# FFN down projection: 2x2 blocks as seven block products of sums in place of eight, four quads in each pair of column chunks

## The chip, the cores and the metric

One Trainium2 chip, one core. The time is the device time of one execution in microseconds (us). Before the change three executions took 1940.80, 1941.48 and 1941.52 us, median 1941.48.

## The reference, cut to what matters

A block of a language model on x [1, 256, 2048] in float32: an FFN, a mixer (sparse attention beside a gated delta rule), a second FFN, each followed by a layer norm over a residual.

```python
def swiglu(x, w_gate, w_up, w_down):            # w_gate, w_up [2048, 5632], w_down [5632, 2048]
    return (jax.nn.silu(x @ w_gate) * (x @ w_up)) @ w_down

h = layer_norm(DEEPNORM_ALPHA * h + 0.5 * swiglu(h, ffn1_w_gate, ffn1_w_up, ffn1_w_down), ln1_g, ln1_b)
mix = hybrid_mixer(h, w_in, ...)
h = layer_norm(DEEPNORM_ALPHA * h + mix, ln2_g, ln2_b)
h = layer_norm(DEEPNORM_ALPHA * h + 0.5 * swiglu(h, ffn2_w_gate, ffn2_w_up, ffn2_w_down), ln3_g, ln3_b)
```

The change touches the two products with w_down: [256, 5632] x [5632, 2048] each.

## The kernel before, in words

All weights stream through the core once, as units: two K tiles (256 rows of the weight) by 512 columns, 512 KB. SyncE loads a unit into one of eight slots of `raw` (`load_unit`, L316), waiting until the unit that held the slot has been split. ScalarE (ACT) copies it, rounded, to `whi` (`split_hi`, L351); VectorE (DVE) subtracts that from `raw` into `wlo` (`split_lo`, L358); both have three slots. TensorE (PE) multiplies the unit: for each half of the 256 tokens and each K tile three matmuls, activation high by weight high (L370), high by low (L371), low by high (L372), with the activations as stationary operand and 512 weight columns moving. That is 12 matmuls a unit. Each engine walks through the stream in one order written out by hand; semaphores count (`hi_done`, `lo_done`, `unit_used`), and `Stream` works out which count each wait needs. `ring_place` gives the slot of a unit: u % 8 for `raw`; for the three split slots u % 3, but behind the middle of a phase with a remainder the ring turns, so that the next phase can begin in slot 0. There some slots are used again after two units and not three.

In a phase "ffn down" the activations lie in `hT` (44 K tiles, high and low parts, features on the partitions). For each of four chunks of 512 columns 22 units accumulate into `acc0` (two PSUM banks, one for each token half), and DVE adds the banks to `resid` (L843) and takes statistics for the layer norm (L854) between the low parts of the next chunk. The first chunk begins while the last 512 columns of hT are still made: gated by up (L759), transposes on PE behind unit 3 (L740), copy and subtraction to hT (L746, L750). In the last chunk the last six units are split into `edge` slots of their own, and PE takes them first for token half 0 and then for half 1 (`exit_units`), so that the norm of the first tile (`exit_tiles`: resid, statistics, norm_columns L622 and L626, transpose L461, xT L474) runs beside half 1. The `edge` slots lie over parts of hT that are used up by then. Before `exit_tiles` DVE splits three units of the next phase. GpSimd loads the norm's gains over the first part of hT and computes the inverse root.

Of the kernel before, what the change touches and what calls it, by code (L numbers as in the profile page):

```python
# [19 lines left out]
P = 128  # L20
# [6 lines left out]
LEAD = 2  # L27
# [9 lines left out]
class Phase:  # L37


    def __init__(self, name, iters, units, width):  # L40
        self.name, self.iters, self.units, self.width = name, iters, units, width

# [13 lines left out]
class Stream:  # L56
# [14 lines left out]
    @staticmethod  # L71
    def uses(ph, s):
        return sum(ring_place(u, ph.units, RAW_SLOTS) == s for u in range(ph.units))
# [5 lines left out]
    def loaded(self, p, it, u):  # L79

        n = self.phases[p].units
        if u >= n:
            it, u = it + 1, u - n
        s = ring_place(u, n, RAW_SLOTS)
        earlier = sum(ring_place(v, n, RAW_SLOTS) == s for v in range(u))
        return it * (16 * self.uses(self.phases[p], s)) + 16 * (self.loads[p][s] + earlier + 1)

    def freed(self, p, it, u, slots):

        n = self.phases[p].units  # L90
# [7 lines left out]
        else:  # L98
            prev = [v for v in range(n) if ring_place(v, n, slots) == s]
            c = prev[-1] - n + 1 if prev else -n  # L100
            if not over:
                if p > 0:
                    m = self.phases[p - 1].units
# [8 lines left out]
def hybrid_block(nc, x, x_t, ffn1_w_gate, ffn1_w_up, ffn1_w_down, ln1_g, ln1_b, w_in, q_norm_g, kv_norm_g,  # L112
# [29 lines left out]
    DOWN_U = FT // UNIT_KT  # L142
    A_ITERS, C_ITERS = 2, 3
    A_W, C_W = A_COLS // A_ITERS, Z_COLS // (C_ITERS + 1)
    B_ITERS = 3 * BW // BANK
    F1GU, F1D, WA, WZ, WB, WC, WQI, WUQ, WO, F2GU, F2D = range(11)
# [3 lines left out]
        Phase("ffn1 down", OUT_CHUNKS, DOWN_U, BANK),  # L150
# [8 lines left out]
        Phase("ffn2 down", OUT_CHUNKS, DOWN_U, BANK),  # L159
    ])  # L160

    n0 = {F1GU: 0, F1D: 11, WA: 15, WZ: 16, WB: 17, WC: 23, WQI: 26, WUQ: 30, WO: 32, F2GU: 36, F2D: 47}
    n1 = {F1GU: 0, WA: 11, F2GU: 12}

    with ExitStack() as ctx:
# [20 lines left out]
        gated = mz("gated", 88, [P, T, BANK])  # L186
        ln_g = mz("ln_g", 0, [P, D])
# [135 lines left out]
        def split_place(p, it, u):  # L323

            n = st.phases[p].units
            if p in EXITS and isinstance(it, int) and it == st.phases[p].iters - 1:
# [16 lines left out]

        def split_hi(act, p, it, u):
            n, w = st.phases[p].units, cut_width(p, it, u)
            hi, _, s, free = split_place(p, it, u)
            r = ring_place(u % n, n, RAW_SLOTS)
            act.wait_ge(raw_loaded[r], st.loaded(p, it, u))
# [4 lines left out]
        def split_lo(dve, p, it, u):  # L353
            n, w = st.phases[p].units, cut_width(p, it, u)
            hi, lo, s, _ = split_place(p, it, u)
            r = ring_place(u % n, n, RAW_SLOTS)
# [60 lines left out]

        def halves(bank):
            return bank.rearrange("p (k s) -> p k s", k=2)
# [9 lines left out]
        def first_units_pe(pe):  # L429

            for v, (c, k) in enumerate(FIRST):
                if v == 0:
                    pe.wait_ge(sem("xT_lo_first"), 1)
# [137 lines left out]
        def to_xT_act(act, q):  # L571
            if q == 0:
                first_hi(act, slice(0, UNIT_KT), sem("x_first"), sem("xT_hi_first"))
# [18 lines left out]
        def to_xT_dve(dve, q):  # L592
            if q == 0:
                first_lo(dve, slice(0, UNIT_KT), sem("xT_hi_first"), 1, sem("xT_lo_first"))
# [44 lines left out]
        def exit_tiles(dve, e, p, scale):  # L639

            c, units = OUT_CHUNKS - 1, KU if p == WO else DOWN_U
            resid_tile(dve, p, c, scale, units, 0)
# [9 lines left out]
            resid_tile(dve, p, c, scale, units, 1)  # L652
# [3 lines left out]
            else:  # L656
                last_pieces(dve, 1)

# [11 lines left out]
        GU, DN = [F1GU, F2GU], [F1D, F2D]  # L670
        EXITS, ENTRIES = (F1D, WO, F2D), (WA, F2GU)
# [12 lines left out]
        def halved_lo(dve, v):  # L684

            for k, (hi, done) in enumerate(((sem("half_hi"), sem("half_lo")), (hi_done, lo_done))):
                dve.wait_ge(hi, v + 1)
# [3 lines left out]
        def halved_unit_mm(pe, v):  # L691
# [3 lines left out]
            for k in range(UNIT_KT):  # L695
                pe.wait_ge((sem("half_lo"), lo_done)[k], v + 1)
# [10 lines left out]
        def ffn_loads(sp, f, w_gate, w_up, w_down, load_x):  # L707
# [21 lines left out]
            with sp.Fori(0, OUT_CHUNKS) as c:  # L729
                for u in range(DOWN_U):  # L730
                    load_unit(sp, DN[f], c, u, down_v[:, 2 * u:2 * u + 2, bass.ds(c * BANK, BANK)])
# [29 lines left out]
        def ffn_pe(pe, f):  # L761
# [20 lines left out]
            def down(c, tail, units):  # L782
                for u in range(units):
                    if tail and u == 0:
                        pe.wait_ge(sem("hT_lo"), (f + 1) * GATE_CHUNKS - 1)
                    if tail and 4 * (GATE_CHUNKS - 1) == 2 * u:
                        pe.wait_ge(sem("hT_lo"), (f + 1) * GATE_CHUNKS)
                    unit_mm(pe, DN[f], c, u, acc0, acc0_free, c + n0[DN[f]], "w", hT, 2 * u, u == 0,
                            u == DOWN_U - 1, acc0a_done)
                    if tail and u == 3:  # L790
                        hT_pe(pe, f, GATE_CHUNKS)

            down(0, True, DOWN_U)
            with pe.Fori(1, OUT_CHUNKS - 1) as c:
                down(c, False, DOWN_U)
            by_tile = (EDGES, LAST_STAGGER)[f]
            down(OUT_CHUNKS - 1, False, DOWN_U - by_tile)
            exit_units(pe, DN[f], hT, by_tile, (1, None)[f])

        def ffn_act(act, f, last):  # L800
# [24 lines left out]
            def down(c, tail, lead):  # L825
                for u in range(LEAD, DOWN_U + lead):
                    split_hi(act, DN[f], c, u)
                    if u == 6 and tail:
                        hT_act(act, f, GATE_CHUNKS)

            down(0, True, LEAD)
            with act.Fori(1, OUT_CHUNKS - 1) as c:
                down(c, False, LEAD)
            down(OUT_CHUNKS - 1, False, 0 if last else SPLIT_SLOTS)

        def resid_add(dve, p, c, scale, in_phase, t):

            cols = bass.ds(c * BANK, BANK)
            if t == 0:
                dve.wait_ge(acc0a_done, c + (n0[p] + 1))  # L840
# [29 lines left out]
        def ffn_dve(dve, f, last):  # L870
# [26 lines left out]
            def down(c, tail, lead):  # L897
                if tail:
                    gate_times_up(dve, f, GATE_CHUNKS)
                for u in range(LEAD, DOWN_U + lead):  # L900
                    split_lo(dve, DN[f], c, u)
                    if u == 6 and tail:
                        hT_dve(dve, f, GATE_CHUNKS)
# [1404 lines left out]
```

## Time and profile before

| | before |
|---|---|
| median of three executions | 1941.48 us |
| span of the profiled execution, first to last instruction | 1939.2 us |
| time of the profiled execution around its span | not shown |
| PE, PEld busy | 99%, 84% |
| DVE, ACT, POOL busy | 57%, 43%, 3% |
| granted PE clock, mean | 0.999 |
| memory traffic | 357 MB, 184 GB/s |

PE is matmul, PEld the weight load that overlaps it. A busy time is the union of an engine's instructions. A matmul's duration in the profile contains its pipeline; the distance of two starts is what one costs in a row of many. An idle time stands with the engine and line that ended it.

### The profile page before, as it was taken

How to read it: one execution, taken by the hardware profiler on the slowest of the kernel's cores; microseconds unless marked ns; L12 is line 12 of the kernel's file. 1: busy time of each engine (PE TensorE's matmuls, PEld its weight loads, DVE VectorE, ACT ScalarE, POOL GpSimd, SP SyncE). 2: the span in 40 equal slices, each digit the busy share in tenths (PEclk: the TensorE clock that was granted, in tenths of full speed). 3: DMA queues.
4: the chain of work that ended last, by engine and by line, in shares of the span. 5: the costliest groups of instructions: out<-in, count | busy, mean ns of one | idle time of the engine just before them, and what ended most of it. 6: DMA issues, size and time to landing. Idle time of an engine off the chain costs nothing.

```text
span 1939.2 us, 28553 instructions
## 1 busy us (share of the span) xinstructions
PE 1922.9 (99%) x10574; PEld 1635.3 (84%) x10574; DVE 1098.2 (57%) x1261; ACT 838.9 (43%) x942; POOL 66.9 (3%) x93
## 2 busy tenths in 40 slices
PE   9999999999999999999999999999999999999997
PEld 8888888888888888999999888888888888888886
DVE  5555554555454456667766958555555555544455
ACT  5444443444333343545744534434444444433332
POOL 0000000000000001300131000000000000000000
PEclk9999999999999999999999999999999999999999
DMA  8666666666655575665432067566666666555663
GB/s 305 194 186 191 187 184 192 176 193 211 212 199 192 191 246 138 212 186 155 128 131 92 20 227 246 166 188 180 189 191 194 193 186 191 187 169 193 202 204 142
DMA packets 185359, 357.29 MB, mean 184 GB/s; under 512 B 11328, under 2 KB 23616, under 8 KB 184272
## 3 DMA queue, kind: packets, MB, share of 16 engines
q1 hardware_dynamic: 183600, 347.43, 57.5%
q0 software_dynamic: 1696, 8.99, 1.4%
q8 instruction: 43, 0.70, 0.2%
q14 instruction: 20, 0.16, 0.0%
HBM read 354.28 MB, written 2.10 MB: 184 GB/s over the span
## 4 chain that ended last, share of the span: by engine, by line
PE 97%; DVE 1%; issue 1%; ACT 0%; DMA 0%; POOLq 0%; POOL 0%; ACTq 0%; DVEq 0%
PE acc L370 27%; PE acc L372 27%; PE acc L371 27%; PE acc L393 3%; PE acc L395 3%; PE acc L397 3%; PE tp L740 1%; PE tp L2087 1%; PE acc L2028 1%; PE acc L2115 0%; PE tp L461 0%; PE acc L2096 0%; DVE wlo L358 0%; PE tp L1970 0%; PE acc L1916 0%
## 5 line engine op out<-in xcount | busy, mean ns | idle before, releaser
L358 DVE TENSOR_TENSOR wlo<-raw,whi 128x1024 fp32r<-128x1024 f32 (+2 forms) x635 | 759.8, 1204 | 758.6 <-ACT whi L351 757.7
L351 ACT ACTIVATE whi<-raw 128x1024 fp32r<-128x1024 f32 (+2 forms) x635 | 654.3, 1039 | 934.1 <-PE acc L372 871.5
L370 PE MATMUL acc<-whi,xT 128*128 128x512 f32 (+2 forms) x1644 | 630.7, 384 | 0.8 <-ACT zab L1203 0.4
L372 PE MATMUL acc<-whi,xT 128*128 128x512 f32 (+2 forms) x1644 | 625.9, 381 | 0.0
L371 PE MATMUL acc<-wlo,xT 128*128 128x512 f32 (+2 forms) x1644 | 625.3, 380 | 0.0
L370 PEld LDWEIGHTS acc<-whi,xT 128*128 128x128 f32 x1644 | 308.7, 188 | 64.7 <-issue 1.7
L372 PEld LDWEIGHTS acc<-whi,xT 128*128 128x128 f32 x1644 | 308.7, 188 | 59.3
L371 PEld LDWEIGHTS acc<-wlo,xT 128*128 128x128 f32 x1644 | 308.9, 188 | 56.0
L370 PE MATMUL acc<-whi,hT 128*128 128x512 f32 x656 | 256.4, 391 | 0.0
L372 PE MATMUL acc<-whi,hT 128*128 128x512 f32 x656 | 255.4, 389 | 0.0
L371 PE MATMUL acc<-wlo,hT 128*128 128x512 f32 x656 | 255.3, 389 | 0.0
L370 PEld LDWEIGHTS acc<-whi,hT 128*128 128x128 f32 x656 | 123.1, 188 | 28.8 <-DVE resid L843 1.8
L372 PEld LDWEIGHTS acc<-whi,hT 128*128 128x128 f32 x656 | 123.1, 188 | 26.0
L371 PEld LDWEIGHTS acc<-wlo,hT 128*128 128x128 f32 x656 | 123.2, 188 | 24.8
L393 PE MATMUL acc<-xT,whi 128*128 128x256 f32 x384 | 108.7, 283 | 0.0
L395 PE MATMUL acc<-xT,whi 128*128 128x256 f32 x384 | 108.7, 283 | 0.0
L397 PE MATMUL acc<-xT,wlo 128*128 128x256 f32 x384 | 108.7, 283 | 0.0
L395 PEld LDWEIGHTS acc<-xT,whi 128*128 128x128 f32 x384 | 73.7, 192 | 0.0
L397 PEld LDWEIGHTS acc<-xT,wlo 128*128 128x128 f32 x384 | 73.7, 192 | 0.0
L393 PEld LDWEIGHTS acc<-xT,whi 128*128 128x128 f32 x384 | 73.7, 192 | 0.0
L662 POOL DMA_DIRECT2D ln_g<-in_ln_g_dram x3 | 1.9, 641 | 1429.0 <-PE acc L372 1429.0
L351 ACT ACTIVATE edge<-raw 128x1024 fp32r<-128x1024 f32 (+1 forms) x30 | 30.0, 1034 | 13.9 <-PE acc L372 11.9
(302 smaller groups left out, 1257.4 us busy)
## 6 DMA issues: line engine op xcount, KB each, us to landing
raw<-in_ffn_w_down_dram SPq DMA_DIRECT2D x176, 512.0 KB, 4.5
raw<-in_ffn_w_up_dram SPq DMA_DIRECT2D x175, 512.0 KB, 3.7
raw<-in_ffn_w_gate_dram SPq DMA_DIRECT2D x174, 512.0 KB, 3.8
raw<-in_w_in_dram SPq DMA_DIRECT2D x48, 512.0 KB, 4.0
raw<-in_w_out_dram SPq DMA_DIRECT2D x32, 512.0 KB, 6.1
raw<-in_w_in_dram SPq DMA_DIRECT2D x32, 260.0 KB, 2.8
raw<-in_w_in_dram SPq DMA_DIRECT2D x16, 456.0 KB, 5.2
raw<-in_w_q_idx_dram SPq DMA_DIRECT2D x8, 512.0 KB, 4.0
```

Of the source, the lines that this page charges most:

```text
L351: act.activation(hi[:, s, :, 0:w], raw[:, r, :, 0:w], ACT.Copy).then_inc(hi_done, 1)
L358: dve.tensor_tensor(lo[:, s, :, 0:w], raw[:, r, :, 0:w], hi[:, s, :, 0:w].bitcast(F32), ALU.subtract).then_inc(lo_done, 1)
L370: pe.matmul(o, hi, w_hi[:, s, k, 0:width], start=first and k == 0, stop=False)
L371: pe.matmul(o, hi, w_lo[:, s, k, 0:width], start=False, stop=False)
L372: ins = pe.matmul(o, lo, w_hi[:, s, k, 0:width], start=False, stop=last and k == UNIT_KT - 1)
L393: pe.matmul(o, whi[:, s, k, cols], hi, start=first and k == 0 and c == 0, stop=False, skip_group_check=True)
L395: pe.matmul(o, whi[:, s, k, cols], lo, start=False, stop=False, skip_group_check=True)
L397: ins = pe.matmul(o, wlo[:, s, k, cols], hi, start=False, stop=end, skip_group_check=True)
L662: pool.dma_start(dst[:], src.to_broadcast([P, D])).then_inc(sem("ln_gains"), 16)
L740: ins = pe.transpose(tp[:, k // 2, (k % 2) * S + t * P:(k % 2) * S + t * P + P], gated[:, t, k * P:k * P + P], ident[:])
L2028: ins = pe.matmul(y_bank(t)[rows, cols64(h)], t1[rows, t, h], yinv[rows, t, h], start=True, stop=True)
L2087: ins = pe.matmul(score_bank(i)[:, hh, 0:n], qidxT[:, h, t * P:t * P + P], kidxT[:, 0:n], start=True, stop=True)
```

## The change

The down phase becomes two phases, one for each pair of column chunks (`Pair`). In a pair four quads are formed from eight units of each chunk: `QUADS = [(4 + q, 8 + q) for q in range(4)]` pairs K unit 4+q with K unit 8+q. A quad is the 2x2 block product: token halves x two K units, times two K units x two chunks. It is done with seven products, each of one token block (or a sum of such) by one unit (or a sum of such), 6 matmuls each, in place of eight. The other 14 units of each chunk are multiplied as before, and stand between the products in a written order (items).

- DVE forms four sums of weight tiles for each quad (P5, P7, P6, P4: 128x1024 each), three of them into `sumB`, one in place in `raw`. ACT and DVE split sums like units. A pair has 56 items (28 units, 28 products) where 44 units were.
- In items 2 to 9 of each FFN's first pair DVE and ACT form four sums of token blocks, with high and low parts (`sumA`, over xT, which is used up).
- P1, P5, P6 and P7 accumulate over the four quads in four PSUM banks (`tp`); P2, P3, P4 go into the chunk's own banks. At the end of a pair seven DVE operations (`fold`) add these banks to resid.
- `acc1` holds the second chunk. Both chunks of a pair are open at the same time.
- The raw ring has 44 tiles a pair in the order of `Pair.raws`; a load waits for the low part of the last item that needs the slot (`released_by`), and for a quad that is later than the next item.
- The three split slots go on with `ring_place` over 56 items. The last six items of the second pair lie in `edge` slots.
- The hardware loops over the chunks are gone.

```diff
+class Pair:
+    def __init__(self, quads, first, second, head, groups):
+        self.items, self.raws = [], []
+        units = [(u, 0) for u in first] + [(u, 1) for u in second]
...
+        plain(head)
+        for n, (a, b) in zip(groups, quads):
+            some, units[:n] = units[:n], []
+            q = quads.index((a, b))
+            self.raws += [(a, 0), (a, 1), some[0], (b, 1), some[1], (b, 0), *some[2:]]
+            forms = [("P1", "P5"), ("P7", "P3"), ("P6", "P2"), ("P4",)]
+            for k in range(4):
+                if k < len(some):
+                    self.items.append(("unit", *some[k]))
+                self.items += [(form, q, 0) for form in forms[k]]
+        self.tail = len(self.items)
+        plain(len(units))
...
+    QUADS = [(4 + q, 8 + q) for q in range(4)]
+    ENDS = [*range(4), *range(12, DOWN_U)]
+    PAIRS = [Pair(QUADS, ENDS, ENDS, 10, (3, 3, 2, 2)),
+             Pair(QUADS, ENDS, ENDS, 2, (4, 4, 4, 3))]
...
-        Phase("ffn1 down", OUT_CHUNKS, DOWN_U, BANK),
+        Phase("ffn1 down: chunks 0 and 1", 1, len(PAIRS[0].items), BANK, len(PAIRS[0].raws)),
+        Phase("ffn1 down: chunks 2 and 3", 1, len(PAIRS[1].items), BANK, len(PAIRS[1].raws)),
...
+                    if r < RAW_SLOTS and pair == 0:
+                        sp.wait_ge(lo_done, st.freed(p, 0, r, RAW_SLOTS))
+                    elif r < RAW_SLOTS:
+                        before = max(v for v in range(len(PAIRS[0].raws)) if v % RAW_SLOTS == s)
+                        sp.wait_ge(lo_done, st.index(DOWN[f][0], 0, PAIRS[0].released_by(before) + 1))
+                    else:
+                        sp.wait_ge(lo_done, st.index(p, 0, plan.released_by(r - RAW_SLOTS) + 1))
...
+            def form_mm(p, i):
...
+                pe.wait_ge(lo_done, st.index(p, 0, i + 1))
+                for k in range(UNIT_KT):
...
+                    pe.matmul(o, x_hi, w_hi[:, s, k], start=i == touches[0] and k == 0, stop=False)
+                    pe.matmul(o, x_hi, w_lo[:, s, k], start=False, stop=False)
+                    ins = pe.matmul(o, x_lo, w_hi[:, s, k], start=False, stop=i == touches[-1] and k == UNIT_KT - 1)
+                ins.then_inc(unit_used, 1)
...
+            def form_hi(p, i):
+                name, q, _ = plan_of(p).items[i]
+                w_hi, _, s, free = split_place(p, 0, i)
+                if name in MADE:
+                    act.wait_ge(sem("formed"), made(f, p, name, q))
...
+                act.wait_ge(unit_used, free)
+                act.activation(w_hi[:, s], form_raw(p, i), ACT.Copy).then_inc(hi_done, 1)
...
+            def add(p, name, q):
+                if name == "P5":
+                    upper, left = raw_ready(dve, p, a, 1), raw_ready(dve, p, a, 0)
...
+                    dve.tensor_tensor(sumB[:, 0], upper, left, ALU.subtract).then_inc(sem("formed"), 1)
+                if name == "P7":
+                    block, right = raw_ready(dve, p, b, 1), raw_ready(dve, p, a, 1)
+                    dve.tensor_tensor(right, block, right, ALU.subtract).then_inc(sem("formed"), 1)
...
+            def sums(i):
+                if i == 2:
+                    sum_of(1, *block(A_KT, 1))
+                if i == 3:
+                    sum_of(2, *block(B_KT, 1))
+                    dve.wait_ge(sem("formed"), summed(f, "A22"))
+                    sum_made(0, 2, 1, 2, ALU.add)
+                if i == 5:
+                    sum_lo(0, 2)
+                if i == 6:
+                    hT_dve(dve, f, GATE_CHUNKS)
+                    sum_of(0, *block(A_KT, 0))
+                if i == 7:
+                    dve.wait_ge(sem("formed"), summed(f, "A11"))
+                    sum_made(1, 1, 0, 1, ALU.subtract)
+                    sum_made(2, 0, 2, 0, ALU.subtract)
+                if i == 8:
+                    dve.wait_ge(sem("formed"), summed(f, "S2"))
+                    sum_of(2, *block(B_KT, 0))
+                    dve.wait_ge(sem("formed"), summed(f, "A12"))
+                    sum_made(3, 2, 2, 0, ALU.subtract)
+                    sum_lo(1, 1)
+                if i == 9:
+                    sum_lo(2, 0)
+                    sum_lo(3, 2)
...
+            def down_pair(pair):
+                for i in range(LEAD if pair == 0 else 0, len(plan.items)):
+                    what, q, _ = plan.items[i]
+                    after = plan.items[i + 1] if i + 1 < len(plan.items) else ("", 0, 0)
+                    if after[0] == "P1":
+                        add(p, "P5", after[1])
+                    if what == "P5":
+                        add(p, "P7", q)
+                    if what == "P7":
+                        add(p, "P6", q)
+                    if after[0] == "P6":
+                        add(p, "P4", after[1])
+                    if what == "unit":
+                        split_lo(dve, p, 0, i)
+                    else:
+                        form_lo(p, i)
+                    if pair == 0:
+                        sums(i)
+                    if i >= plan.tail:
+                        pair_end(pair, i - plan.tail)
```

`pair_end` adds the first chunk's banks to resid at the tail's items 2 and 3, folds at items 4 to 7, and takes two statistics at item 7; the second chunk's banks follow in items 2 and 3 of the next pair, or in `exit_tiles`.

## Rows read from the trace of the kernel before

**Rows 1.** Page: engines' busy time; granted clock by slices.
```profile
PE 1922.9 (99%) x10574; PEld 1635.3 (84%) x10574; DVE 1098.2 (57%) x1261; ACT 838.9 (43%) x942; POOL 66.9 (3%) x93
...
PEclk9999999999999999999999999999999999999999
```

**Rows 2.** Page: the chain of waits by engine.
```profile
PE 97%; DVE 1%; issue 1%; ACT 0%; DMA 0%; POOLq 0%; POOL 0%; ACTq 0%; DVEq 0%
```

**Rows 3.** Chain of waits, FFN2: start us, us, what; eight transposes of hT.
```profile
1698.29 0.87 PE tp L740 x8
```

**Rows 4.** Window: us; busy (count) of PE, PEld, DVE, ACT, POOL; clock; DMA share.
```profile
1747.00:1807.00 60.00, 60.00 (x266) 49.43 (x265) 29.00 (x26) 23.12 (x22) 0.00 (x0) 1.00 0.60 193
```

**Rows 5.** Timeline of PE, starts of two units: start, duration, instruction.
```profile
1739.70 0.39 PE L372 MATMUL acc<-whi,hT 128*128 128x512 f32 x1
...
1742.42 0.39 PE L372 MATMUL acc<-whi,hT 128*128 128x512 f32 x1
```

**Rows 6.** Groups, FFN2 down: busy, mean ns, idle before and its releaser.
```profile
L358 DVE TENSOR_TENSOR wlo<-raw,whi 128x1024 fp32r<-128x1024 f32 x80 | 97.2, 1224 | 108.1 <-ACT whi L351 108.1
...
L351 ACT ACTIVATE whi<-raw 128x1024 fp32r<-128x1024 f32 x80 | 84.0, 1059 | 135.4 <-PE acc L372 135.4
```

**Rows 7.** Timeline, change of unit.
```profile
1748.09 0.39 PE L370 MATMUL acc<-whi,hT 128*128 128x512 f32 x1
...
1748.28 1.06 ACT L351 ACTIVATE whi<-raw 128x1024 fp32r<-128x1024 f32 x1 [1.60 <-PE acc L372]
```

**Rows 8.** Timeline, a slot used again after two units.
```profile
1778.11 0.39 PE L370 MATMUL acc<-whi,hT 128*128 128x512 f32 x1
...
1778.30 2.01 ACT L351 ACTIVATE whi<-raw 128x1024 fp32r<-128x1024 f32 x2 [4.38 <-PE acc L372]
...
1779.40 2.36 DVE L358 TENSOR_TENSOR wlo<-raw,whi 128x1024 fp32r<-128x1024 f32 x2 [4.21 <-ACT whi L351]
...
1780.68 0.19 PEld L370 LDWEIGHTS acc<-whi,hT 128*128 128x128 f32 x1
...
1780.84 0.40 PE L370 MATMUL acc<-whi,hT 128*128 128x512 f32 x1
```

**Rows 9.** Timeline of DVE without a pause.
```profile
716.99 3.49 DVE L358 TENSOR_TENSOR edge<-raw,edge 128x1024 fp32r<-128x1024 f32 x3
```

**Rows 10.** Timeline of DVE, FFN2 down: its start, and the end of PE's work.
```profile
1687.44 1.28 DVE L759 TENSOR_TENSOR gated<-gated,acc 128x512 f32<-128x512 f32 x2 [0.40 <-PE acc L372]
...
1688.65 1.22 DVE L358 TENSOR_TENSOR wlo<-raw,whi 128x1024 fp32r<-128x1024 f32 x1
...
1699.48 1.23 DVE L358 TENSOR_TENSOR wlo<-raw,whi 128x1024 fp32r<-128x1024 f32 x1 [1.50 <-ACT whi L351]
...
1700.62 1.22 DVE L750 TENSOR_TENSOR hT<-tp,hT 128x1024 fp32r<-128x1024 f32 x1
...
1928.52 0.69 DVE L843 SCALAR_TENSOR_TENSOR resid<-acc,resid 128x512 f32<-128x512 f32 x1 [0.73 <-PE acc L372]
```

**Rows 11.** Timeline, chunk boundary.
```profile
1746.92 0.69 DVE L843 SCALAR_TENSOR_TENSOR resid<-acc,resid 128x512 f32<-128x512 f32 x1 [1.70 <-PE acc L372]
...
1749.27 1.27 DVE L854 BATCH_NORM_STATS2 stats<-resid 128x6 f32<-128x512 f32 x2
...
1749.40 0.19 PEld L370 LDWEIGHTS acc<-whi,hT 128*128 128x128 f32 x1 [0.22 <-DVE resid L843]
```

**Rows 12.** FFN1's exit: timeline; next phase's loads (KB, median us to landing).
```profile
727.67 0.69 DVE L843 SCALAR_TENSOR_TENSOR resid<-acc,resid 128x512 f32<-128x512 f32 x1 [1.86 <-PE acc L372]
...
730.70 0.75 DVE L626 SCALAR_TENSOR_TENSOR resid<-resid,rstd,ln_b 128x512 f32<-128x512 f32 x1 [0.47 <-POOL rstd L667]
...
732.91 0.60 PE L461 MATMUL tp<-ident,resid 128*128 128x128 f32 x4
...
raw<-in_w_in_dram SPq DMA_DIRECT2D x11, 456.0 KB, 5.3
```

**Rows 13.** Window in the mixer, small groups on PE, columns as in rows 4.
```profile
1020.00:1055.00 35.00, 33.63 (x590) 32.11 (x591) 19.33 (x32) 15.72 (x27) 3.96 (x4) 1.00 0.31 99
```

More of the change, by code:

```diff
@@ L72, in uses @@
     def uses(ph, s):
-        return sum(ring_place(u, ph.units, RAW_SLOTS) == s for u in range(ph.units))
+        return sum(ring_place(u, ph.raws, RAW_SLOTS) == s for u in range(ph.raws))
     def index(self, p, it, u):
@@ L79, in loaded @@
     def loaded(self, p, it, u):
[L81 removed]
+        n = self.phases[p].raws
         if u >= n:
@@ L88, in freed @@
     def freed(self, p, it, u, slots):
-        n = self.phases[p].units
+        n = self.phases[p].places(slots)
         over = u >= n
@@ L102, in freed @@
                 if p > 0:
-                    m = self.phases[p - 1].units
+                    m = self.phases[p - 1].places(slots)
                     prev = [v for v in range(m) if ring_place(v, m, slots) == s]
@@ L342, in split_place, with edge_free, plan_of, raw_unit @@
             return whi, wlo, ring_place(u % n, n, SPLIT_SLOTS), st.freed(p, it, u, SPLIT_SLOTS)
+        def edge_free(slot):
+            plan = PAIRS[1]
+            over = (4 + 2 * slot, 5 + 2 * slot)
+            return 1 + max(i for i, (what, x, _) in enumerate(plan.items)
+                           if (x in over if what == "unit" else not set(over).isdisjoint(plan.quads[x])))
+        def plan_of(p):
+            return {F1DA: PAIRS[0], F1DB: PAIRS[1], F2DA: PAIRS[0], F2DB: PAIRS[1]}.get(p)
+        def raw_unit(p, u):
+            return u if plan_of(p) is None else plan_of(p).raw_of(u)
         def split_hi(act, p, it, u):
@@ L657, in exit_tiles, with gains_free @@
                 last_pieces(dve, 1)
+        def gains_free(f):
+            return st.index(DOWN[f][1], 0, 1 + PAIRS[1].last(*(("unit", u, 1) for u in range(KT // 4))))
         def norm_gains(pool, g, b):
@@ L780, in ffn_pe @@
                 gate_up(c, True)
[L782 to L790, printed above, removed]
-                        hT_pe(pe, f, GATE_CHUNKS)
@@ new lines, in down_unit @@
+            def down_unit(p, i):
+                plan = plan_of(p)
+                _, u, c = plan.items[i]
+                acc, free, n = ((acc0, acc0_free, n0), (acc1, acc1_free, n1))[c]
+                if p == DOWN[f][0] and 2 * u >= 4 * (GATE_CHUNKS - 1):
+                    pe.wait_ge(sem("hT_lo"), hT_all)
+                pe.wait_ge(lo_done, st.index(p, 0, i + 1))
+                for half in range(2):
+                    touches = plan.touches((c, half))
+                    if i == touches[0]:
+                        pe.wait_ge(free[half], n[p])
+                    ins = token_mm(pe, p, 0, i, acc, half, hT, 2 * u, i == touches[0], i == touches[-1])
+                ins.then_inc(unit_used, 1)
@@ new lines, in ffn_pe @@
+            for p in DOWN[f]:
+                plan = plan_of(p)
+                n = len(plan.items) - (EDGES if p == DOWN[f][1] else 0)
+                for i in range(n):
+                    if p == DOWN[f][0] and i == 0:
+                        pe.wait_ge(sem("hT_lo"), hT_all - 1)
+                    if plan.items[i][0] == "unit":
+                        down_unit(p, i)
+                    else:
+                        form_mm(p, i)
+                    if p == DOWN[f][0] and i == 3:
+                        hT_pe(pe, f, GATE_CHUNKS)
@@ L909, in ffn_dve, with last_tile @@
             if f == 0:
                 dve.wait_ge(sem("x_resid"), 16)
-            down(0, True, 0)
-            with dve.Fori(1, OUT_CHUNKS - 1) as c:
-                down(c, False, 0)
-            down(OUT_CHUNKS - 1, False, 0 if last else SPLIT_SLOTS)
+            gate_times_up(dve, f, GATE_CHUNKS)
+            for pair in range(2):
+                down_pair(pair)
+            for u in range(0 if last else SPLIT_SLOTS):
+                split_lo(dve, F1DB, 0, len(PAIRS[1].items) + u)
+            def last_tile(t):
+                down_add(1, 1, t)
+                down_stats(1, 1, t)
```

314 lines of the change are left out of this document (260 added, 54 removed).

## The prediction

> **What bounds the kernel now.** I read the page's busy row first, then the chain of waits, then the two down projections by windows. PE is busy for 99% of the span at the full clock, and 97% of the chain is PE; DVE works 57% and ACT 43% [rows 1, 2]. In a window of one down chunk's length PE has no hole at all, while DVE is busy for 29.0 of 60.0 us [rows 4]. A unit (256 of the K rows, 512 columns) starts at 1739.70 and the next at 1742.42 [rows 5]: 12 matmuls in 2.72 us, so 0.227 us each. The 0.39 us of a matmul's own duration overlaps its neighbours and is no price. Idle time of DVE in front of the low parts is ended by ACT, that of ACT by PE [rows 6]: the weights are split only as PE gives slots back. So what counts is (a) matmuls and (b) whether the next item is split when PE wants it.
>
> **Matmuls removed.** A quad replaces two units of each column chunk: 4 x 12 = 48 matmuls become 7 products x 6 = 42. Four quads in each of two pairs and two FFNs take away 96. 96 x 0.227 = 21.8 us, all on PE. The chunk boundary of before holds the next chunk's weight load at 1749.40 until DVE has emptied the bank [rows 11]; a down stage takes 241.0 us (from 1687.3, where gate and up end, to 1928.3, just before DVE's last waits end [rows 10]), and 1056 x 0.2269 + 0.87 for eight transposes [rows 3] make 240.5. I take these losses, 2 x 0.5, as gone. Together -22.8 us.
>
> **What a split costs in time.** PE's next unit starts at 1748.09, ACT at 1748.28 (the slot was given back 0.03 us before) [rows 7]. ACT takes 1.06, DVE starts 0.04 later and takes 1.23, and PE can load 0.05 after that. The whole loop is seen where before has two-slot spacing: unit 11 starts at 1778.11, the low part of unit 12 starts at 1779.40, its weight load comes at 1780.68 and its matmul at 1780.84 [rows 8]. So a slot that PE gives up on starting item i+1 serves an item 2.73 us after that start at the earliest. With three slots the two items between must last 2.72 us together. Before, they last 5.44. Two products (1.36 each) last 2.72: no reserve at all, and whatever DVE does in front of that low part is a stall. Where DVE runs without a pause three operations take 3.49 us, 1.13 from start to start [rows 9]. The new additions have the same shape and engine (128x1024, f32, two SBUF inputs), so I price them at 1.13, between 1.08 (twice what the second 512 of 1024 elements add, 1.23 - 0.69 [rows 8, 11]) and 1.23 (the full duration).
>
> The Trainium skill (VectorE: DVE Perf Modes, "The DRAIN you can't avoid") says that the next operation does not start until the pipe is empty, though one that is not held starts earlier. Here the trace shows the latter: 1.13 against a duration of 1.23. By the stricter reading the time would be the third rival's.
>
> **Slots two apart.** 56 items in three slots leave remainder 2, so the ring turns behind the middle: item 29 takes the slot of 27, item 30 that of 28. In the first pair the items before them are P2 and P4, in the second P7 and P3: products. Each must wait 2.72 instead of 1.36: 2 x 1.36 a pair, 4 pairs: 10.9 us. Only the measured loop stands behind this, no backlog.
>
> **DVE's order in a quad.** Relative to P5's start at 0: low of U (-0.07), P6's addition 1.06, low P7 2.19, low P3 3.32, P4's addition 4.45, low U 5.58, PE may go on at 5.58 + 1.43 = 7.01; PE is there at 6.80: 0.2 stall. In the two short quads P4's addition comes before low P3, whose PE time is 5.44: ready at 4.45 + 1.43 = 5.88, 0.44 stall. At the join of two quads in the first pair the order is low P4, P5's addition, low U. Low P4 starts 1.29 after P6's start, so U is ready at 1.29 + 2 x 1.13 + 1.43 = 4.98, PE at 3 x 1.36 = 4.08: 0.9 stall. It comes at joins 1 and 3 (the slot stall covers join 2). The second pair has a unit in front of P4, so no join stall.
>
> **The token sums.** Twelve operations over hT are put into items 2 to 9 of each FFN's first pair, on DVE, with four copies on ACT. With item 0 at 0 (1687.3) and 0.88 for the transposes, items start at 11.8 (4), 14.5, 17.2, 19.9, 22.7, 25.4, 28.1 (10). Low 2 runs at 1.3 and low 6 with hT at 12.2 to 14.4 as before [rows 10]. Then hT's A11 sum; low 7 at 15.8, two sums, low 8 at 19.2, two sums and a low part, low 9 at 23.9, two low parts, P5's addition 27.5 (each own result waited for adds 0.1), low 10 at 28.6: ready 30.0 against 28.1. 1.9 stall. Bounds 0 (DVE has 14 us of pause before item 6 that an earlier start could use) and 3 (1.23 each).
>
> First pair: 1.9 + 0.2 + 0.9 + 0.2 + 2.72 + 0.44 + 0.9 + 0.44 = 7.7.
>
> **Second pair and its end.** Three quads with 0.2 (the slot stall covers the fourth), 2.72, and the tail: the folds of the product banks (seven operations, 0.6 to 0.68 for 512 elements as the bank reads and statistics of before [rows 11], 1.13 for the wide one) and two statistics fall between low 47 and low 53, where PE's items have become half units of 1.36. With item 45 at 0: low 49 at 6.7, low 50 9.2, low 51 11.4, low 52 13.8, low 53 17.5, ready 18.9, PE at 17.7: 1.2. Sum 4.5. At the end of the first pair the same folds have full units of 2.72 beside them and cost nothing.
>
> **Hand-over of FFN1.** 44 raw tiles in eight slots leave 4, so the next phase's first tile waits for the low part of item 52, its second and third for 53 and 54 (before: six back, and split early). A load lands 5.3 us after issue (median) [rows 12]. On the clock above: issued 18.7 and 19.9, landed by 24 and 25, high and low parts on ACT and DVE until 26.9, and only then the first tile's addition, which PE's half makes possible at 23.0 + 0.2. Before it started at 727.67 and the norm's output was there at 731.45, the transpose at 732.91 [rows 12]: 1.4 reserve. 26.9 - 23.2 - 1.4 = 2.3, with the queue's spread 2.5. Bounds 0 and 4. The same start at four raw slots between the pairs is covered: first tile issued at 8, wanted at 16.5. Within quads every raw tile is issued at least 7 us before use. The end of FFN2 has no such loads; its tail is unchanged.
>
> **Sum.** Stalls 2 x (7.7 + 4.5) + 2.5 = 26.9; gains 22.8. +4.1 us. Span 1939.2 becomes 1943.3. The profile gives no time around its span; the median of the runs, 1941.48, lies 2.3 above it. 1941.5 + 4.1 = 1945.6.
>
> **Rivals.**
> 1. DVE keeps up: additions and sums fit into its pauses and only slots two apart cost. For it: DVE would work about 56 x 1.13 + 16 x 1.13 + sums per 183 us, under half. Against: the pauses are in the plain units, the additions in the quads (14 operations x 1.13 = 15.8 us in 17.7 us of PE, 13 in 15.0). -22.8 + 10.9 = -11.9: 1929.6. It decides when a quad's joins show no PE hole. With joins (3.6) 1933.
> 2. The full saving, all stalls covered (ACT and DVE run ahead of my rule, because the slots come free sooner than at an item's end): 1918.7. Against it stands the loop in [rows 8].
> 3. DVE pays 1.23 each: the sum stall grows to 2.9, the 0.2 to 0.7, 0.44 to 0.84, 0.9 to 1.1, the end 1.2 to 2.2. Pairs 10.9 and 7.0, hand-over 3: 38.8 - 22.8 = +16: 1957.5. For it: dependent operations (a wait for one's own result) do pay it. Against: [rows 9].
> 4. Late loads: the four tiles held for a quad and bursts behind them; one load's 5.3 us late by 1 us at each of 16 quads: +16 on the forecast's 4, 1961. Against: DMA is at 0.6 of its share in these windows [rows 4].
> 5. The clock. Short PE holes come 6 to 9 a pair. In a stretch with PE busy for 33.6 of 35 us in small groups the granted clock stayed 1.00 [rows 13]. If it fell to 1.2 GHz for all 672 product matmuls, 672 x 0.227 = +152 us more. The Trainium skill (TensorE: Matmul & The Clock Gate, "A second HAM failure mode: psum-queue depth-cycling") tells of just this, idle moments between groups that cycle PSUM banks making the clock swing; the trace speaks against it so far.
>
> **Chances.** Forecast 0.55 (own range 1940 to 1951, slightly more than half of it above 1945.4), rival 1 0.18, rival 2 0.04, rival 3 0.15, rival 4 0.06, rival 5 0.02. A difference under 0.2%, 3.9 us, can't be told from none. Faster: 0.18 + 0.04 + 0.01 of the forecast's = 0.23. Same: 0.25. Slower: 0.29 + 0.15 + 0.06 + 0.02 = 0.52. Range 1934 to 1954: it takes in the forecast, most between it and rival 1, and half of rival 3.
>
> **What would show it.** 96 fewer 128x512 matmuls; PE waiting for the low part (not for raw) about 1.3 us in front of items 29 and 30 of each pair, about 0.9 at the joins of the first pair, about 2 at its first quad; in FFN1 the first tile's addition 3 to 4 us after PE's half, with ACT's last high parts waiting for DMA. DVE's pitch in quads 1.13. I am wrong if items 29 and 30 show no hole (the loop is shorter than I read), or if PE's holes in the pairs sum to less than 18 or more than 35 us.

## The result, and the profile after

| | before | after |
|---|---|---|
| median | 1941.31 us (14 runs) | 1945.53 us (14 runs, 1944.82 to 1948.55) |
| ratio to before | | 1.0024, 95% interval [1.0016, 1.0031] |
| span of the profiled execution | 1939.2 us | 1943.1 us |

Slower by 4.2 us, 0.24%, and clear of noise by the interval. The forecast was 1945.6. Of the 14 runs after, twelve lie below 1946; the other two took 1947.73 and 1948.55 us with a mean granted clock of 0.997, and no trace of them is kept. The page's busy row after:

```profile
PE 1909.5 (98%) x10478; PEld 1613.9 (83%) x10478; DVE 1269.0 (65%) x1425; ACT 900.8 (46%) x1002; POOL 66.9 (3%) x93
```

The records of PE fell by exactly 96, as counted (before: [rows 1]). Busy time fell by 13.4 us only: a matmul whose weights come late stands longer in the record. DVE has 164 more operations. By the starts of the same instructions, from the first of the last eight transposes of hT to DVE's last addition of a bank, FFN1's stage went from 231.4 to 234.2 us and FFN2's from 230.4 to 231.4. Forecast were +3.3 and +0.8; measured +2.8 and +1.0. The spans of the two profiled executions differ by 3.9 us: 0.3 us more comes before FFN1's down stage and 0.2 us is gained back in the mixer; the cause of both is open.

DVE is far busier in this stage than over the whole kernel. In a stretch of FFN2's down stage, 1701 to 1900 us (columns as in [rows 4]), it works for 169.77 of 199 us, 85%, against 48% in the window of before:

```profile
1701.00:1900.00 199.00, 191.94 (x833) 153.12 (x832) 169.77 (x154) 105.89 (x102) 0.00 (x0) 1.00 0.57 190
```

In the chain of waits by engine (compare [rows 2]) 7 points of PE have become DVE, ACT and issue.

```profile
PE 90%; DVE 6%; issue 2%; ACT 1%; DMA 0%; POOL 0%; POOLq 0%; ACTq 0%; DVEq 0%
```

What PE waited for (us in total, times, longest). Before had none of these in the down stages:

```profile
PE acc L463 <- DVE wlo L451: 8.4, 10, 1.7
PE acc L985 <- DVE wlo L1173: 5.7, 8, 1.2
PE tp L574 <- DVE resid L739: 1.7, 1, 1.7
PE acc L463 <- DVE edge L451: 1.6, 2, 0.8
```

L463 is the first matmul of a unit, L985 that of a product, L451 the low part of a unit and L1173 that of a product; L574 is the transpose in FFN1's exit. Nothing there names raw: the quads' loads are in time.

Item 29 (P4) and item 30 (a unit) of FFN2's first pair in the timeline, with start and duration (compare [rows 8]):

```profile
1754.78 1.06 ACT L1054 ACTIVATE whi<-sumB 128x1024 fp32r<-128x1024 f32 x1 [3.26 <-PE tp L987]
1755.87 1.23 DVE L1173 TENSOR_TENSOR wlo<-sumB,whi 128x1024 fp32r<-128x1024 f32 x1 [3.10 <-ACT whi L1054]
1756.14 1.06 ACT L444 ACTIVATE whi<-raw 128x1024 fp32r<-128x1024 f32 x1 [0.30 <-PE acc L987]
1757.02 1.22 DVE L1156 TENSOR_TENSOR sumB<-raw 128x1024 f32<-128x1024 f32 x1
...
1757.15 0.50 PE L985 MATMUL acc<-whi,hT 128*128 128x512 f32 x1 [1.11 <-DVE wlo L1173]
1758.15 1.22 DVE L451 TENSOR_TENSOR wlo<-raw,whi 128x1024 fp32r<-128x1024 f32 x1
...
1759.42 0.50 PE L463 MATMUL acc<-whi,hT 128*128 128x512 f32 x1 [0.60 <-DVE wlo L451]
```

ACT stands idle for 3.26 us until PE gives back the slot of item 27; then come 1.06 and 1.23 us, and only then PE. That is the loop of the prediction. Item 30 is different from the forecast: ACT starts it at 1756.14, when item 28 ends and before PE has begun item 29. What holds PE there is P5's addition (L1156) between the two low parts.

A hole is time in which PE stands although it has work left. The table gives the holes in FFN2 in us, from the distances of starts less 0.227 us, with the 0.1 us by which the next matmul is late too:

| place | forecast | after |
|---|---|---|
| behind the token sums | 1.9 | 1.9 |
| joins 1 and 3, first pair | 0.9, 0.9 | 0.9, 0.9 |
| item 29, first and second pair | 1.36, 1.36 | 1.4, 1.4 |
| item 30, first and second pair | 1.36, 1.36 | 0.9, 0.8 |
| P3 of the short quads | 0.44, 0.44 | 0.5, 0.5 |
| units behind P3 (five) | 0.2 each | 0.1 to 0.2 each |
| second pair's end | 1.2 | 1.1 |

The whole stage lost 12.3 us by the distance between the transposes of hT and the first tile's addition, less the 0.227 of each matmul; forecast 12.2.

FFN1's exit (compare [rows 12]): ACT's last three high parts of the next phase wait for their raw tiles, and DVE's addition of the first tile comes at 732.1, where before had it at 727.7, so the transposes wait:

```profile
724.27 1.06 ACT L444 ACTIVATE whi<-raw 128x1024 fp32r<-128x1024 f32 x1 [3.46 <-DMA raw<-in_w_in_dram]
728.00 1.06 ACT L444 ACTIVATE whi<-raw 128x1024 fp32r<-128x1024 f32 x1 [2.66 <-DMA raw<-in_w_in_dram]
729.88 1.06 ACT L444 ACTIVATE whi<-raw 128x1024 fp32r<-128x1024 f32 x1 [0.82 <-DMA raw<-in_w_in_dram]
...
732.12 0.68 DVE L1233 SCALAR_TENSOR_TENSOR resid<-acc,resid 128x512 f32<-128x512 f32 x1
...
736.03 0.63 PE L574 MATMUL tp<-ident,resid 128*128 128x128 f32 x4 [1.67 <-DVE resid L739]
```

### The profile page after: what moved, and what is told of

It reads as the page before. It is cut to its first block, busy times and chain, and to the rows that moved or that the text cites. A ratio compares the mean times of both kernels' runs of the same rounds, so it can differ in the third digit from the quotient of the medians.

```text
span 1943.1 us, 28005 instructions
## 1 busy us (share of the span) xinstructions
PE 1909.5 (98%) x10478; PEld 1613.9 (83%) x10478; DVE 1269.0 (65%) x1425; ACT 900.8 (46%) x1002; POOL 66.9 (3%) x93
## 4 chain that ended last, share of the span: by engine, by line
PE 90%; DVE 6%; issue 2%; ACT 1%; DMA 0%; POOL 0%; POOLq 0%; ACTq 0%; DVEq 0%
PE acc L463 23%; PE acc L465 23%; PE acc L464 23%; PE acc L486 3%; PE acc L490 3%; PE acc L488 3%; DVE wlo L451 1%; PE tp L987 1%; PE tp L985 1%; PE tp L986 1%; PE tp L917 1%; PE acc L985 1%; PE acc L987 1%; PE acc L986 1%; ACT whi L444 1%
## 5 line engine op out<-in xcount | busy, mean ns | idle before, releaser
L451 DVE TENSOR_TENSOR wlo<-raw,whi 128x1024 fp32r<-128x1024 f32 (+1 forms) x571 | 682.7, 1201 | 583.7 <-ACT whi L444 581.3
L444 ACT ACTIVATE whi<-raw 128x1024 fp32r<-128x1024 f32 (+1 forms) x571 | 588.1, 1037 | 794.2 <-PE acc L465 713.6
L463 PE MATMUL acc<-whi,xT 128*128 128x512 f32 (+2 forms) x1644 | 631.0, 384 | 0.8 <-ACT zab L1612 0.4
L463 PEld LDWEIGHTS acc<-whi,xT 128*128 128x128 f32 x1644 | 308.7, 188 | 64.7 <-issue 1.8
L463 PE MATMUL acc<-whi,hT 128*128 128x512 f32 x400 | 158.7, 397 | 8.4 <-DVE wlo L451 8.4
L464 PE MATMUL acc<-wlo,hT 128*128 128x512 f32 x400 | 156.0, 390 | 0.0
L465 PE MATMUL acc<-whi,hT 128*128 128x512 f32 x400 | 156.0, 390 | 0.0
L463 PEld LDWEIGHTS acc<-whi,hT 128*128 128x128 f32 x400 | 75.0, 188 | 35.0 <-DVE wlo L451 17.2
L465 PEld LDWEIGHTS acc<-whi,hT 128*128 128x128 f32 x400 | 75.1, 188 | 16.1
L464 PEld LDWEIGHTS acc<-wlo,hT 128*128 128x128 f32 x400 | 75.2, 188 | 14.0
L1054 ACT ACTIVATE whi<-raw 128x1024 fp32r<-128x1024 f32 x64 | 67.9, 1061 | 36.6 <-PE acc L465 20.7
L1173 DVE TENSOR_TENSOR wlo<-raw,whi 128x1024 fp32r<-128x1024 f32 x64 | 77.3, 1221 | 9.2 <-ACT whi L1054 7.7
```

The costliest lines, as they stand in the source:

```text
L444: act.activation(hi[:, s, :, 0:w], raw[:, r, :, 0:w], ACT.Copy).then_inc(hi_done, 1)
L451: dve.tensor_tensor(lo[:, s, :, 0:w], raw[:, r, :, 0:w], hi[:, s, :, 0:w].bitcast(F32), ALU.subtract).then_inc(lo_done, 1)
L463: pe.matmul(o, hi, w_hi[:, s, k, 0:width], start=first and k == 0, stop=False)
L464: pe.matmul(o, hi, w_lo[:, s, k, 0:width], start=False, stop=False)
L465: ins = pe.matmul(o, lo, w_hi[:, s, k, 0:width], start=False, stop=last and k == UNIT_KT - 1)
L1054: act.activation(w_hi[:, s], form_raw(p, i), ACT.Copy).then_inc(hi_done, 1)
```

## The experiments

All start from the changed kernel (1945.5 us), and "less" is less than that. Each ratio is to the kernel before. Theory A: PE's holes are the loop of 2.73 us and DVE's additions in front of low parts, term by term. Its main rival, B: the amount of work on DVE, wherever it stands. C and D are named in the expectations. Four runs begin.

**e1_ring**, the split ring's turn where the items are full units:

```diff
-    middle = max(1, units // 2)
+    middle = 50 if units == 56 else max(1, units // 2)
```

> The turn of the split ring is moved from behind item 28 (products) to behind item 50 (full units, edge items in the second pair). Theory A (the loop of 2.73 us from a slot given back to the next matmul, plus 1.13 us for each addition that DVE does in between): item 29's hole of 1.4 us goes in all four pairs; item 30's 0.85 us stays in the first pair, since P5's addition stands in front of it, and shrinks to 0.1 to 0.2 in the second. 4 x 1.4 + 2 x 0.65 = 6.9 us less than the changed kernel: about 1938.6. Theory B (DVE has too much work in the quads, wherever the slots turn): the holes move to the following items, under 2 us gained, above 1943.5.

Measured 1944.73 us (1943.78 to 1945.37), ratio to before 1.0018 [1.0009, 1.0028]: 0.8 less, where 6.9 were expected. A miss, and the number lies where theory B put it. The trace shows more. The holes at item 29 are gone in all four pairs, and item 30 is 0.9 in the first and 0.1 to 0.2 in the second pair, as theory A says. But the second pair began with new ones, 2.5 us in FFN2 and 3.1 in FFN1, behind a late raw tile:

```profile
1816.35 1.06 ACT L444 ACTIVATE whi<-raw 128x1024 fp32r<-128x1024 f32 x1 [4.99 <-DMA raw<-in_ffn_w_down_dram]
...
1818.72 0.50 PE L463 MATMUL acc<-whi,hT 128*128 128x512 f32 x1 [0.36 <-DVE wlo L451]
...
1824.85 0.47 PE L985 MATMUL tp<-whi,sumA 128*128 128x512 f32 x1 [1.72 <-DVE wlo L1173]
```

In the changed kernel ACT's wait there was 2.0 us and cost PE nothing. The raw ring has only four tiles of lead at the border; five loads are issued at once when the first pair's last low part is done (here at 1808.6), and this tile, the second of them, landed at 1816.3, 7.7 us after that. In the changed kernel it was there at 1813.9, 6.1 us after. Within the stage PE came to the border 1.4 us earlier, and the stage had begun 0.6 us later; why the tile took longer in this trace is open.

**e2_p5**, P5's addition one item earlier (not for the first quad behind the token sums):

```diff
-                    if after[0] == "P1":
-                        add(p, "P5", after[1])
+                    then = plan.items[i + 2] if i + 2 < len(plan.items) else ("", 0, 0)
+                    late = pair == 0 and i <= 10
+                    if (after if late else then)[0] == "P1":
+                        add(p, "P5", (after if late else then)[1])
```

> P5's weight addition for the next quad is done one item earlier (in front of P4's low part, where the profile shows DVE idle, and not between it and the unit's). Same work on every engine. Theory A: joins 1 and 3 of the first pair lose 0.94 and 0.89 us, item 30's 0.86 goes too: 2 x 2.7 = 5.4 us less, about 1940.1; the second pair does not change. Theory B (DVE's amount of work): the same holes within 1 us, above 1944.5. Theory C (PE pays for the change between products and units): no change either.

Measured 1941.20 us (1940.59 to 1942.48), ratio 1.0000 [0.9990, 1.0009]: 4.3 less. The holes at both joins and at item 30 of the first pair are gone; in front of P4 of the short quads stand 0.4 us that were not foreseen (the addition now delays P4's low part there). PE's waits for the low part of a unit (8.4 us, 10 times) are these now:

```profile
PE acc L463 <- DVE wlo L451: 4.5, 4, 1.7
```

The same work on DVE at another place is worth 4.3 us, which B does not allow. The trace shows one thing more, by windows of FFN1's exit (columns as in [rows 4], the granted clock the third from the end):

```profile
732.00:734.00 2.00, 0.32 (x2) 0.00 (x0) 1.50 (x4) 0.00 (x0) 1.00 (x1) 1.00 1.05 397
...
735.00:736.00 1.00, 1.00 (x4) 0.75 (x3) 1.00 (x2) 0.53 (x1) 0.00 (x0) 0.50 1.05 405
...
740.00:744.00 4.00, 4.00 (x21) 3.62 (x20) 3.79 (x7) 0.59 (x1) 2.28 (x3) 1.00 0.08 8
```

Behind a hole of 2.1 us in front of the transposes PE worked at 0.50 of its clock, 1.2 GHz, for some 3 us; matmuls came every 0.43 us and not every 0.23, which cost some 1.5 us. The profiled execution is the slowest of the ten (1942.48 us against a median of 1941.20), so the median need not contain this.

**e3_late**, two low parts of the next phase behind the first tile's norm:

```diff
                 norm_tile(dve, e, 1, 0)
+                if e == 0:
+                    for u in range(1, SPLIT_SLOTS):
+                        split_lo(dve, F1DB, 0, len(PAIRS[1].items) + u)
...
-            for u in range(0 if last else SPLIT_SLOTS):
+            for u in range(0 if last else 1):
                 split_lo(dve, F1DB, 0, len(PAIRS[1].items) + u)
```

> At FFN1's exit two of the three low parts of the next phase (whose raw tiles land late) are done behind the first tile's norm and not in front of it. If the 1.8 us in front of the transpose and the 0.4 behind come from the late raw tiles through DVE's order: the transpose does not wait, but 2.3 us of DVE come in front of the first xT parts, of which up to 0.7 may show in the entry: 1.5 us less (0.7 to 2.2), about 1944.0. If it was PE's transposes waiting for the folds of the banks instead: no change.

Measured 1944.34 us (1943.92 to 1944.84), ratio 1.0016 [1.0006, 1.0025]: 1.2 less. There is no hole in front of the transposes. Two of 0.4 us stand in the entry; one of them is in before and in the changed kernel too, so 0.4 us is new. This trace also shows how little reserve the border of the pairs has: nothing was changed up to there, but the same tile landed 6.7 us after its issue and not 5.7, ACT waited 2.9 us for it, and PE stood for 0.5 us.

**e4_tiny**, the additions on 8 of 512 columns of each K tile, so that most of each weight sum is not formed while every wait, split, product and load stays:

```diff
-                    dve.tensor_tensor(sumB[:, 0], upper, left, ALU.subtract).then_inc(sem("formed"), 1)
+                    dve.tensor_tensor(sumB[:, 0, :, 0:8], upper[:, :, 0:8], left[:, :, 0:8], ALU.subtract).then_inc(sem("formed"), 1)
```

and so for P7, P6 and P4.

> The 64 weight additions work on 16 of 1024 columns only, so the sums of weight tiles are not formed; every wait, split, product and load stays. Theory A: of 12.3 us of holes in each down stage about 4.7 stay (0.8 behind the token sums, 1.4 at item 29 in both pairs, 1.1 at the exit): 2 x 7.6 = 15 us less, about 1930.4, and item 30 shows no hole. Theory C (PE pays for products as such, or for its extra waits): no change. Theory D (raw tiles are late in the quads): no change or less than 2 us.

Measured 1932.61 us (median of 5, of which one took 3883.02 and the others 1932.45 to 1933.85), ratio 0.9958 [0.9942, 0.9974]: 12.9 less, where 15 were expected. Of FFN2's holes those at item 29 (1.4, 1.4), the exit's 1.1 and 0.9 behind the sums are left; joins, item 30 and P3 of the short quads are clean. Together these are some 5 us, and 6.2 us by all distances of starts; the expectation left out the small ones. So products, their extra waits and the bank changes cost PE nothing by themselves (C and D fall), and the additions cost nearly 13 us. This run alone does not part A from B, since it takes work from DVE as well; the places of the holes that went do, and e2_p5 and e6_ring_raw with all the work left.

The next two runs take the raw ring, alone and with e1_ring's edit. **e5_raw**:

```diff
     def uses(ph, s):
-        return sum(ring_place(u, ph.raws, RAW_SLOTS) == s for u in range(ph.raws))
+        return sum((ph.shift + u) % RAW_SLOTS == s for u in range(ph.raws))
...
+        def raw_slot(p, v):
+            ph = st.phases[p]
+            return (v + ph.shift) % RAW_SLOTS if v < ph.raws else (v - ph.raws) % RAW_SLOTS
```

with shift 4 for the second pairs, wherever a raw slot is worked out.

> The raw ring of the second pair starts at slot 4, so that it goes on without a break behind the 44 tiles of the first and in front of the next phase: a phase's first tile waits for the tile eight before it, not four. Nothing else changes. If the hand-over of FFN1 (1.8 and 0.4 us of PE) is the late raw tiles: both go, ACT shows no wait of over 0.3 us for a raw tile at either border: 2.0 us less than the changed kernel, about 1943.5. If it is DVE's chain at the exit whatever the loads: no change.

Measured 1943.27 us (1943.00 to 1944.27), ratio 1.0011 [1.0001, 1.0021]: 2.3 less. The hole in front of the transposes is gone; the 0.4 us in the entry, which the expectation counted in, stays, as in before. ACT's waits at the exit shrank from 3.46, 2.66 and 0.82 us to one of 0.16:

```profile
722.05 2.26 ACT L451 ACTIVATE whi<-raw 128x1024 fp32r<-128x1024 f32 x2 [0.16 <-DMA raw<-in_w_in_dram]
```

**e6_ring_raw**, the edits of e1_ring and e5_raw.

> e1_ring and e5_raw together. In the run of e1_ring the holes at item 29 were gone in all pairs, but the second pair began with new ones (0.5 and 1.9 in FFN2, 1.1 and 1.9 in FFN1), in front of which ACT waited 5.0 us for a raw tile. Theory A2 (the removed slot stalls were real, and were given back at the border because the raw ring has only four tiles there): with both, the 6.9 us of the slots and the 2.2 of the hand-over come: about 1936.5. Theory B (DVE's amount of work brings the holes back wherever): above 1941.

Measured 1936.67 us (1936.47 to 1937.04), ratio 0.9976 [0.9966, 0.9985]: 8.9 less, where each alone gave 0.8 and 2.3. The waits for low parts of products (5.7 us, 8 times, longest 1.2 in the changed kernel) have lost item 29:

```profile
PE acc L992 <- DVE wlo L1180: 1.0, 4, 0.3
```

No wait for a raw tile is left at the pairs' border. e1_ring's miss is settled: the slots' 6.9 us were real (6.6 beside e5_raw) and had mostly been given back at the border. B expected more than 1941.

**e8_dve**:

```diff
-    PAIRS = [Pair(QUADS, ENDS, ENDS, 10, (3, 3, 2, 2)),
+    PAIRS = [Pair(QUADS, ENDS, ENDS, 11, (3, 2, 2, 2)),
...
                 if i == 9:
                     sum_lo(2, 0)
+                if i == 10:
                     sum_lo(3, 2)
...
-                if i == 7:
+                if i == (7, 10)[pair]:
                     for t in range(T):
                         down_stats(pair, 0, t)
```

> Only two of the edits on the changed kernel: statistics behind the last edge item, and one more unit in front of the first quad (groups 3, 2, 2, 2) with the last low part one item later. The hole of 1.1 us at the exit and that of 1.9 us behind the token sums go to under 0.3; the second quad gets the 0.5 of a short quad for 0.2. 2 x (1.1 + 1.2) = 4.5 us less: about 1941.0. If the hole behind the sums is not their backlog on DVE but the wait for hT or for the product banks: it stays.

Measured 1940.94 us (1940.18 to 1942.37), ratio 0.9998 [0.9988, 1.0008]: 4.6 less. The hole behind the sums fell from 1.9 to 0.3, and the exit's 1.1 is gone. In FFN1 the hole in front of the transposes grew from 1.8 to 2.1 us, and behind it the granted clock was at 0.50 for some 3 us in this trace, which is that of the slowest of the ten executions.

**e12_p5_raw**, the edits of e2_p5 and e5_raw.

> e2_p5 with the raw ring without a break. e2_p5 gained 4.3 of 5.4 us; its trace has the granted clock at 0.50 for 3 us behind a hole of 2.0 us in front of FFN1's transposes, where the changed kernel's hole was 1.7 and the clock stayed at 1.00. If this fall was what was missing: without that hole the clock stays at 1.00 there, and the gains are 5.4 (P5) and 2.2 (raw) below 1945.5: about 1937.9. If P5's move itself gives only 4.3: 1939.0.

Measured 1938.54 us (1938.30 to 1939.05), ratio 0.9988 [0.9978, 0.9997]: between the two. The clock stays at 1.00 and there is no hole in front of the transposes. Beside e5_raw P5's move gives 4.7 us, beside the changed kernel 4.3. So the exit, with its clock, accounts for some 0.4 us of what is missing to 5.4. P4's new hole, 0.4 us in two short quads of each FFN and 1.7 in all, stands in both traces and covers the rest; some smaller holes have shrunk beside it.

**e7_all**, all of e2_p5, e6_ring_raw and e8_dve.

> All edits: split ring's turn at item 50, raw ring without a break, P5's addition one item earlier, the end's two statistics of the second pair behind the last edge item, and one more unit in front of the first quad with the last low part of the token sums one item later. Sum by the measured holes: slots 6.9, joins and item 30 of the first pair 5.4 (4.3 were measured), hand-over 2.2, exit's 1.1 twice, token sums 1.2 twice (1.9 less 0.3 that stays less 0.4 for a quad with one unit less): 18.9 us below 1945.5, 1926.6, between 1924 and 1931. Theory B (work of DVE): not under 1934.

Measured 1928.78 us (1928.70 to 1929.77), ratio 0.9937 [0.9920, 0.9953]: 16.8 less than the change, 12.5 less than before. 18.9 were expected. The trace has 0.4 us in front of P4 in each of the six short quads, 2.4 in all, which the sum had left out, and 0.9 in front of FFN1's transposes. **e10_late** is e7_all with e3_late's edit.

> e7_all with two of the three low parts of the next phase behind the first tile's norm at FFN1's exit (the edit of e3_late). In e7_all 0.9 us of PE stand in front of the transposes there, from the statistics that were moved behind the edge items. This hole goes; 0.4 may come in the entry behind it: 0.3 to 0.9 less than e7_all, about 1928.2.

Measured 1928.45 us (1928.06 to 1928.72), ratio 0.9935 [0.9919, 0.9952]. It is the best version here, though 0.3 us below e7_all is little against the spread of four executions each. Its first wait of PE in the down stages is this, the six short quads:

```profile
PE acc L995 <- DVE wlo L1183: 1.6, 6, 0.3
```

DVE is as busy as in the changed kernel, 173.85 us in the same stretch against 169.77, and yet PE stands for little more than 1 us there and not for 7. That is the plainest case against B:

```profile
1701.00:1900.00 199.00, 197.89 (x857) 158.42 (x857) 173.85 (x160) 110.55 (x107) 1.10 (x2) 1.00 0.60 202
```

**e9_pool**, e7_all with P4's addition on GpSimd:

```diff
+                for q, (a, b) in enumerate(PAIRS[DOWN[f].index(p)].quads):
+                    left = raw_ready(pool, p, b, 0)
+                    pool.wait_ge(sem("formed"), made(f, p, "P6", q))
+                    pool.tensor_tensor(sumB[:, 2], left, sumB[:, 1], ALU.subtract).then_inc(sem("pool_made"), 1)
```

> e7_all with P4's weight addition on GpSimd, which is idle in the down stages; DVE has one operation of 1.13 us less in each of 16 quads. Theory A (PE's remaining holes are additions in front of low parts): in each FFN the 0.5 in front of P3 of the three short quads, their 0.4 at the next product and the 0.2 in front of units go, 2.5 to 3 us a stage: 5 to 6 us less than e7_all, about 1923.5. Rival: GpSimd and DVE disturb each other in SBUF, so that an addition on GpSimd (2.6 us by two 512-column operations of 1.32 in the trace of before) stretches DVE's 1.22 us operations: no gain or slower than 1928.8.

Measured 1948.46 us (1948.19 to 1948.90), ratio 1.0039 [1.0025, 1.0053]: 19.7 slower than e7_all. The rival won. Timeline, GpSimd's addition and DVE beside it:

```profile
1748.55 4.56 DVE L1190 TENSOR_TENSOR wlo<-raw,whi 128x1024 fp32r<-128x1024 f32 x2
```

```profile
1748.78 3.25 POOL L902 TENSOR_TENSOR sumB<-raw,sumB 128x1024 f32<-128x1024 f32 x1 [16.18 <-DVE sumB L1183]
```

The two low parts took 4.56 us; two in a row took 2.36 [rows 8]. By single records the first, which had started before GpSimd's addition, kept its 1.22 us; the second took 3.42 and ended 1.1 us after GpSimd did, and so in all 16 quads. DVE lost 2.2 us to save 1.13, and PE stood for 1.5 us in front of P3 in every quad. **e11_pool_late** adds e3_late's edit.

> e9_pool and e10_late together: the sum of both gains, about 1923 if GpSimd does not disturb DVE.

Measured 1948.17 us (1947.86 to 1948.48), ratio 1.0037 [1.0022, 1.0051]: the same loss.

## Why the prediction was right

- **Matmuls removed:** 96 records less; 21.8 us. FFN2's stage gives this to 0.1 us when the holes are added back: 12.3 us of holes, less 10.9 for the matmuls and the 0.5 of before, is +0.9; measured +1.0.
- **The loop of 2.73 us:** right at item 29 in all pairs, shown by e1_ring, where those holes went, and e6_ring_raw, where the time went with them.
- **Slots two apart, 2 x 1.36 a pair:** the second half was mis-sized and had the wrong cause. "Each must wait 2.72 instead of 1.36" counted for item 30 from the start of item 29. The slot is free when item 28 ends, and PE was idle between the two. Measured 0.8 to 0.9, from the addition in front of its low part while DVE is late from item 29; e4_tiny has none there, e2_p5 none in the first pair, and e1_ring, without the stall of item 29, 0.1 to 0.2 in the second. In the sum 2 x 1.0 us too much.
- **DVE's order in a quad, 1.13 each:** joins 0.9, short quads 0.44 and the 0.2 came as worked out; e2_p5 moved the joins away with the amount of work unchanged. Additions are recorded with 1.22 us, 1.13 from start to start in a row. The third rival (1.23) is out.
- **Token sums 1.9:** 1.9; e8_dve shows it to be backlog.
- **The end of the second pair 1.2:** 1.1.
- **Hand-over 2.5:** 1.8 in front of the transposes, so 0.7 too much; e5_raw shows the cause, four tiles of raw lead. The expectations of e3_late and e5_raw count 0.4 behind the transposes to it; before has the same 0.4 there.
- **"The same start at four raw slots between the pairs is covered":** right for this kernel, with less reserve than it seemed. ACT waited 2.0 us, PE not at all. Only the phase's first tile was worked out, with a median landing time of 5.3 us. The late one is the second of five issued in one burst: it landed 5.7 us after its own issue in the changed kernel and 7.3 in e1_ring. e1_ring's expectation failed on this.
- **DVE's load, in rival 1:** "under half" was wrong. A pair's 28 units and 28 products take 28 x 2.72 + 28 x 1.36 = 114 us of PE, not 183, and 72 x 1.13 = 81 us of DVE without the sums is 71% of that; measured 85%. The forecast did not use this number, but it made rival 1 look better than it was.
- **Rivals:** 1 and 2 need joins and item 29 without holes; there are such holes. 4: no raw wait in the quads. 5: the clock never fell in the pairs, whose holes are 1.9 us at most. It fell at FFN1's exit in the traces of e2_p5 and e8_dve, behind holes of 2.1 us, and not in the changed kernel's trace, with 1.8.

The closeness of the sum is partly luck: 2 us too much at item 30 and 0.7 at the hand-over stand against small holes of 0.02 to 0.1 us that were left out, some 1 us a stage, and the 0.3 us in front of FFN1's.

## What to carry to other kernels

When arithmetic is taken from a busy engine by giving its helper more steps, work out the loop from "slot given back" to "next work ready" and compare it with the shortest two or three items in a row, not with the mean load. Here DVE was busy for 65% of the whole and 85% of the down stages; in the changed kernel the 22 us saved were lost to its order, and in e10_late, with DVE no less busy, most of them were not. Then move additions to where the helper is idle and let no ring turn or restart among short items; the same seven products then gained 12.9 us over the kernel before.
Where a hole is removed, check what the next border has in reserve: one gain of 6.9 us showed as 0.8 until the load ring was mended too.

## What the hardware showed

- A two-input 128x1024 f32 operation of DVE, 1.22 us alone, took 3.42 us when it came up while GpSimd ran a two-input addition of the same size (3.25 us), and ended 1.1 us after GpSimd: DVE stood until GpSimd had finished. The one already running when GpSimd began kept 1.22 (e9_pool, all 16 times). Offloading one of four additions made the kernel 20 us slower.
- In front of FFN1's transposes holes of 1.8 us (the changed kernel, e4_tiny) and 2.0 us (e1_ring) left the granted clock at 1.00; holes of 2.1 us (e2_p5, e8_dve) were followed by some 3 us at 0.50. These are five traces, too few to call it a bound.
- Of five 512 KB loads issued within 2.1 us at the border of FFN2's pairs (the changed kernel), the first landed 3.9 us after its issue, the next ones 5.7, 9.0, 9.6 and 10.4. The median of all loads of w_down was 4.9 us.
- After each hole of FFN2's down stage (0.2 to 1.8 us, eleven in the changed kernel) PE's second matmul came another 0.1 us late.
